# One 4 MB weight load of a mixture-of-experts kernel, made as a load of 96 rows and four loads of 8 rows

## What is computed

```python
D_MODEL, SEQ, N_EXPERTS, TOP_K, D_FF = 1024, 256, 32, 4, 1024

def moe_ffn(x, g_ffn, w_router, b_router, w_mlp1, b_mlp1, w_mlp2, b_mlp2):
    xt = rms_norm(x, g_ffn).reshape(N, D)
    logits = (xt @ w_router + b_router).astype(jnp.float32)
    top_v, top_e = lax.top_k(logits, TOP_K)
    wts = jax.nn.softmax(top_v, axis=-1).astype(x.dtype)
    ...
    def expert_block(args):
        xblk, e = args
        hdn = xblk @ w_mlp1[e] + b_mlp1[e]
        x_glu = jnp.minimum(hdn[:, ::2], SWIGLU_LIMIT)
        x_lin = jnp.clip(hdn[:, 1::2], -SWIGLU_LIMIT, SWIGLU_LIMIT)
        act = x_glu * jax.nn.sigmoid(SWIGLU_ALPHA * x_glu) * (x_lin + 1.0)
        return act @ w_mlp2[e] + b_mlp2[e]
    ...
    return x + y.reshape(B, S, D)
```

## Time and profile before

| | us |
|---|---|
| median of 3 runs | 1176.12 |
| lowest and highest of them | 1175.56, 1177.36 |
| the profiled execution | 1175.9 |
| its span (first to last instruction) | 1174.1 |
| PE busy in the span | 1126.4 (96%) |
| DVE, ACT, POOL busy | 399.8, 227.9, 26.8 |
| all DMAs | 454.37 MB, mean 387 GB/s |
| issue to landing of a 4 MB load (raw, median of 12) | 40.8 |

### The profile page before, as it was taken

One profiled execution on the slowest core, in us unless ns is written; L12 is line 12 of the kernel. 1 busy time (PEld: TensorE's weight loads), 2 busy tenths in 40 slices (PEclk: granted clock), 3 DMA queues, 4 the chain that ended last, 5 costly groups with the idle time before them and its releaser, 6 DMA issues.

```text
span 1174.1 us, 13010 instructions
## 1 busy us (share of the span) xinstructions
PE 1126.4 (96%) x5300; PEld 528.6 (45%) x5300; DVE 399.8 (34%) x664; ACT 227.9 (19%) x355; POOL 26.8 (2%) x38
## 2 busy tenths in 40 slices
PE   9999999999999999999999989999999999999998
PEld 8888788873333333333333333333333333333332
DVE  4765656753232222322322222222222222222221
ACT  3555557441000000101100000000000000000001
POOL 0001221010000000000000000000000000000000
PEclk9999999999999999999999999999999999999999
DMA  9866547998999999999999999999999999999995
GB/s 349 306 204 232 162 161 260 386 391 347 414 416 425 426 432 433 430 434 430 433 429 428 435 431 430 429 431 429 431 435 430 429 428 433 425 427 428 427 428 243
DMA packets 45633, 454.37 MB, mean 387 GB/s; under 512 B 3824, under 2 KB 4080, under 8 KB 27152
## 3 DMA queue, kind: packets, MB, share of 16 engines
q1 hardware_dynamic: 45008, 452.12, 92.9%
q10 hardware_dynamic: 576, 1.51, 0.3%
HBM read 452.56 MB, written 1.05 MB: 386 GB/s over the span
## 4 chain that ended last, share of the span: by engine, by line
PE 70%; DMA 29%; DVE 0%; issue 0%; ACT 0%; SPq 0%
PE PS L1733 23%; PE PS L1489 16%; PE PS L1740 13%; DMA gate_raw<-in_w_mlp 7%; DMA head_raw<-in_w_mlp 7%; DMA value_raw<-in_w_mlp 6%; DMA low_raw<-in_w_mlp 6%; DMA raw<-in_w_mlp 4%; PE PS L1776 3%; PE PS L1679 2%; PE PS L1456 1%; PE PS L1520 1%; PE PS L1763 1%; PE PS L1686 1%; PE PS L1429 1%; PE PS L1503 1%
## 5 line engine op out<-in xcount | busy, mean ns | idle before, releaser
L974 ACT ACTIVATE hT<-hT 128x512 f32<-128x512 f32 x31 | 19.5, 630 | 535.9 <-DVE hT L1389 535.9
L1389 DVE TENSOR_SCALAR hT<-PS 128x512 f32<-128x512 f32 x32 | 22.1, 692 | 296.8 <-PE PS L1733 296.8
L1733 PE MATMUL PS<-head_raw,XG 128*64 128x512 f32 x432 | 95.8, 595 | 4.3 <-DMA head_raw<-in_w_mlp 4.3
L1316 DVE TENSOR_TENSOR XG<-PS,gains 128x512 f32<-128x512 f32 x31 | 21.4, 692 | 225.0 <-PE PS L1686 225.0
L1733 PE MATMUL PS<-value_raw,XG 128*64 128x512 f32 x416 | 92.1, 595 | 3.0 <-DMA value_raw<-in_w_mlp 3.0
L1051 DVE TENSOR_TENSOR rest<-raw,mix_hi 128x2048 fp32r<-128x2048 f32 x35 | 80.2, 2291 | 43.0 <-ACT mix_hi L807 43.0
L1733 PE MATMUL PS<-low_raw,XG 128*64 128x512 f32 x400 | 89.0, 595 | 5.4 <-DMA low_raw<-in_w_mlp 5.4
L1733 PE MATMUL PS<-raw,XG 128*64 128x512 f32 x384 | 84.9, 595 | 4.5 <-DMA raw<-in_w_mlp 4.5
L1733 PE MATMUL PS<-gate_raw,XG 128*64 128x512 f32 x384 | 85.3, 595 | 3.1 <-DMA gate_raw<-in_w_mlp 3.1
L1328 DVE TENSOR_TENSOR hx<-hx,PS 128x512 f32<-128x512 f32 x116 | 72.2, 683 | 42.3 <-PE PS L1776 42.3
L807 ACT ACTIVATE mix_hi<-raw 128x2048 fp32r<-128x2048 f32 x35 | 67.0, 1914 | 40.3 <-PE PS L1489 26.2
(11 more groups left out here) (291 smaller groups left out, 1237.1 us busy)
## 6 DMA issues: line engine op xcount, KB each, us to landing
low_raw<-in_w_mlp SPq DMA_DIRECT2D x12, 4096.0 KB, 38.8
value_raw<-in_w_mlp SPq DMA_DIRECT2D x12, 4096.0 KB, 38.5
raw<-in_w_mlp SPq DMA_DIRECT2D x12, 4096.0 KB, 40.8
head_raw<-in_w_mlp SPq DMA_DIRECT2D x12, 4096.0 KB, 40.3
gate_raw<-in_w_mlp SPq DMA_DIRECT2D x11, 4096.0 KB, 40.3
value_raw<-in_w_mlp SPq DMA_DIRECT2D x14, 2048.0 KB, 25.4
low_raw<-in_w_mlp SPq DMA_DIRECT2D x14, 2048.0 KB, 25.5
head_raw<-in_w_mlp SPq DMA_DIRECT2D x13, 2048.0 KB, 14.0
```

Of the source, the lines that this page charges most:

```text
L974: act.activation(sig, glu, ACT.Sigmoid, scale=ALPHA).then_inc(sgm, 1)
L1316: dve.tensor_tensor(XG[:, :, :].rearrange("p (h c) s -> p h c s", h=2), banks[4].rearrange("p (c h s) -> p h c s", h=2, s=SL), rowgain.to_ ...
L1389: dve.tensor_scalar(glu, PS[:, 0:1024:2], LIMIT, None, ALU.min).then_inc(swi, 1)
L1733: mm = pe.matmul(PS[h * SL:(h + 1) * SL, n * 512:(n + 1) * 512], XG[:, 2 * u + c, :], parts[n].rearrange("p (q h r) -> p h q r", h=2, r=8) ...
```

## The change

The load `("up", 26, 2)`, 4 MB into the tile `raw`, is made by a new function, `load_w1_pair_uneven`: rows 0 to 95 in one DMA, which has the semaphore of the old one, and rows 96 to 127 in four DMAs of 8 rows each, which add to a new semaphore `uneven_in`. PE waits for both before `up(26, 2)`; `up(26, 3)` needs no new wait, since it comes later on PE. Nothing else is different, and all other loads and all arithmetic stay.

```diff
--- before.py
+++ after.py
@@ -85,6 +85,7 @@
 HALVES = [LOADS[LATER + i] for i in range(4)]
 HALF_RELEASED = FIRST[:4]
 PAIRS_END = 27
+UNEVEN = ("up", PAIRS_END - 1, 2)
 B2_BEFORE = LOADS[LATER + SLOTS_N]
 LAST_BANK = {(0, 0): 4, (0, 1): 3, (1, 0): 7, (1, 1): 5}
 SLOT = {load: HOMES[n] for n, load in enumerate(FIRST)}
@@ -413,6 +414,7 @@
 
         raw_in = [sem(f"raw_in{i}") for i in range(MIX_RING)]
         ring_in = [sem(f"ring_in{i}") for i in range(SLOTS_N)]
+        uneven_in = sem("uneven_in")
         half_used, half_in = sem("half_used"), [sem(f"half_in{i}") for i in range(len(HALVES))]
         first_half = {load: sem(f"first_half{i}") for i, load in enumerate(TWO_ROWS)}
         apart_in = {(load, c): sem(f"apart_in{i}{c}") for i, load in enumerate(APART) for c in range(2)}
@@ -545,6 +547,12 @@
 
             def load_w1_pair(e, u, pair, landed):
                 sp.dma_start(pair[:, :], w1[e, 256 * u:256 * u + 512, :].rearrange("e (p k) n -> p (e k n)", k=4)).then_inc(landed, 16)
+
+            def load_w1_pair_uneven(e, u, pair, landed):
+                rows = w1[e, 256 * u:256 * u + 512, :].rearrange("e (p k) n -> p (e k n)", k=4)
+                sp.dma_start(pair[0:96, :], rows[0:96, :]).then_inc(landed, 16)
+                for q in range(96, P, 8):
+                    sp.dma_start(pair[q:q + 8, :], rows[q:q + 8, :]).then_inc(uneven_in, 16)
 
             def load_w2_pair(e, pair, landed):
                 sp.dma_start(pair[:, :], w2[e, :, :].rearrange("e (p k) n -> p (e k n)", k=8)).then_inc(landed, 16)
@@ -693,7 +701,9 @@
                 used(held_before(n + in_pairs(load)))
                 tile, landed, _ = weight_tile(kind, j, u)
                 if in_pairs(load):
-                    if kind == "up":
+                    if load == UNEVEN:
+                        load_w1_pair_uneven(slice(j, j + 1), u, pairs[SLOT[load] // 2], landed)
+                    elif kind == "up":
                         load_w1_pair(slice(j, j + 1), u, pairs[SLOT[load] // 2], landed)
                     else:
                         load_w2_pair(slice(j, j + 1), pairs[SLOT[load] // 2], landed)
@@ -1718,6 +1728,8 @@
                     if load in TWO_ROWS:
                         pe.wait_ge(first_half[load], 16)
                     pe.wait_ge(landed, count)
+                    if load == UNEVEN:
+                        pe.wait_ge(uneven_in, 4 * 16)
                 for c in range(2):
                     if load in APART:
                         pe.wait_ge(apart_in[load, c], 32 if c == 0 else 16)
```

## The result

The changed kernel takes **1205.68 us** (median of 5 runs, 1201.4 to 1208.76); the kernel before, on the same chip, 1176.12 (median of 5, 1175.38 to 1179.24). The ratio is 1.0249, with a 95% interval of 1.0234 to 1.0264: 29.6 us slower. The forecast was 1192.5, with a range of 1177 to 1200. The direction was right, the size was not.

A forecast was written before the change was run, and what follows sets the result against it. Queued weight transfers were taken as the bound. On the serving engines 7.3 + 24.4 - 9.8 = 21.9 us, less a lead of 5.5, gave 16.4 us later: 1176.1 + 16.4 = 1192.5 us, range 1177 to 1200.

The forecast's parts named there:

- What bounds the kernel: From 906 us on, queued weight transfers at 429 GB/s are the bound; a delay reaches the end one for one.
- A row in an 8-row load, 4.9 to 6.1 us: In the four 8-row loads on eight engines, each 32 KB row takes this long; full rate is 1.22 us.
- The carry-over from 32 rows to 8: 32-row loads ran at half rate; in proportion 8 rows get an eighth, 54 GB/s, 19.5 us for the four loads.
- The 96-row load, 7.3 us or at most 9.8: Six rows per engine at 1.22 us, or 9.8 if 64 of the rows take only half the stream.
- The sum before the lead, 21.9 us: Extra time on the serving engines: 7.3 for 96 rows plus 24.4 for four 8-row loads, less 9.8 before.
- The subtraction of the lead, 5.5 us: Half the engines finish 4 to 7 us before the others; if they serve the 8-row loads, 5.5 us is covered.
- Issues on SP, 2.0 us, covered: Four more DMA issues at half a us each, hidden in the 10.7 us before SP's next issue, head_raw.
- The wait on PE near 997, 15 us or more: Sign in the profile after: one PE wait for raw of this length, where it had been 1.5 us.
- The plateau with the other half late: Sign at the end of the loads: half the engines busy for longer than 4 us, the former leading half now late.
- Balanced: Rival: 8-row loads at full rate on the leading half, landings 2.4 us earlier, 1173.7 us; chance 0.13.
- milder limit: Rival: a row in an 8-row load takes 2.4 us, end 1.8 us later, 1177.9 us; chance 0.07.
- wrong half: Rival: 8-row loads at full rate on the already late half, 2.4 us later, 1178.5 us; chance 0.04.

The follow-up runs named there:

- The early kernel: Changed kernel with the same uneven load made at item 8 instead of item 26: 1197.59 us, ratio 1.0195 to the kernel before.
- Alone: Loads-only kernel, no layer computed, each pattern awaited before the next: 128 rows 12.1 us, rows 0 to 95 16.8, four 8-row loads of neighbours 19.4.
- in line: Loads-only kernel, five 4 MB loads issued at once, the third changed: plain 51.1 us, with 96 rows and four 8-row loads 77.8.
- 96 + 32 rows: Changed kernel with one load of rows 96 to 127 in place of the four 8-row loads: 1193.31 us, ratio 1.0151 to the kernel before.
- the columns kernel: Changed kernel with its load as five loads of all 128 rows, half of each row, then four of 4 KB of each: 1175.83 us, ratio 0.9999.
- The last runs: Kernel before, load cut into every-fourth-row loads plus four or eight 8-row loads: rows 16 apart 1185.49, 1195.77 us; 4 apart 1181.84, 1186.29; sixteen, 16 apart, 1214.07.
- 64 + 64 rows: Kernel before with the load at item 26 made as rows 0 to 63 and rows 64 to 127: 1189.89 us, ratio 1.0122.
- the second series in line: Loads-only kernel, five 4 MB loads issued at once, the third as 96 rows and four 8-row loads: 77.8 us, 26.7 over plain.

## Why the prediction was wrong in size

- **What bounds the kernel**: right. The transfers do, and a delay goes to the end. The early kernel, with a wait of 2.3 us and a loss of 21, is the strongest proof.
- **A row in an 8-row load, 4.9 to 6.1 us**: right in kind and near in size. Alone 4.3 us (17.1/4), and 4.6 where all four go to the same rows; in line behind full loads 5.6, and in the profiled run some 3.8 (median of the 71 rows that start from 996 to 1012 us). The carry-over from 32 rows to 8, which the prediction named as its weak point, held to within a fifth or so.
- **The 96-row load, 7.3 us or at most 9.8**: wrong, and the first step that failed. It takes 14.5 us alone, six rows of 2.4 us on every engine. 96 rows were read as 128 rows less a quarter; a full rate was assumed where no row of the trace had shown one for less than 128 rows. This term alone makes 96 + 32 rows cost 10 us in line and 17.6 in the kernel, with no 8-row load at all.
- **The sum before the lead, 21.9 us**: by the times of the loads alone it would be 14.5 + 17.1 - 9.8 = 21.8. The same number, with one term too small by 7 and the other too large by 7; an accident. In line, where a row of an 8-row load takes 5.6 us, it is 14.5 + 22.3 - 9.8 = 27.0, and 26.7 was measured: there the 24.4 for the four loads is near, and the 7.3 for the 96 rows is what is missing.
- **The subtraction of the lead, 5.5 us**: wrong, the second step that failed. It held that the serving engines fall behind while the others go on. They don't go on at their rate: in the slow stretch the busy share stays at 9 and the rate is at a quarter to a half of full, and no row on any engine takes less than 2.3 us, even of the load ahead (46.7 us from issue to landing, where 41 was usual). In line every row on all 16 engines takes 5.6 us while the 8-row loads run. "The other half of the engines has work for longer than the delay, so it does not stop" was the sentence that made this mistake: it had work, but was slowed down as much. The lead itself was there and of about the size taken: before, the signals of the leading eight for `raw` came at 990.0 to 991.6 us, those of the late eight at 994.7 to 996.6. Which half serves was left open. In the profiled run it was neither: as far as the packets can be joined end to start, six of the eight serving engines are of the leading half and two of the late one. Without the subtraction the forecast would have been 1198; with 26.7, 1202.8, beside 1201.4 measured for the profiled run.
- **Issues on SP, 2.0 us, covered**: right; 1.36 us, covered, and the columns kernel confirms it.
- **The wait on PE near 997, 15 us or more**: right, 22.4, with 4.3 before it that were not foreseen. The 96-row load at its old time or earlier: wrong, 17 us later; the last 8-row load some 20 us after it: wrong, 10.5 us (1014.1 and 1024.6). The share at 1 with a low rate: right. The plateau with the other half late: wrong, there is none.
- **Balanced, milder limit, wrong half**: none of them occurred. The last runs show no form in which shifting rows between the halves gains anything, even with the rows spread. That the change might do nothing is excluded by the result.

What stays open: why a row of a 96-row load takes 2.4 us on every engine, and why the engines without rows of an 8-row load are slowed to its pace, which the runs show without a reason; and the 4 us between the profiled run and the median.

## What to carry to other kernels

A load should cover all 128 rows, and if it must be cut, by columns, or by every fourth row over the whole tile; both cost nothing here, while 96 + 32 or 64 + 64 rows cost 14 to 18 us for one 4 MB load. Few neighbouring rows hold up every transfer that is under way, so no lead or reserve elsewhere pays for them; in a kernel whose loads stand in line, count lost transfer, not waits. A term taken over at full rate because it looked harmless needs its row as much as the one under dispute.

## What the runs showed of the hardware

- Rows 0 to 95 take longer than rows 0 to 127: 16.8 against 12.1 us alone. Rows 0 to 111 do as well: issued at 223.00, the next pattern at 239.29, 16.3 us.
- While 8-row loads of neighbouring rows run among full loads, all 16 engines are busy (share 0.96) and together move 90 GB/s; with a 96-row load it is 218, with full loads 431 (the second series in line).
- Alone, 8 rows at a distance of 4 are at full rate (8.4 us for four loads), at 2, 8 or 16 at half of it (12.2 to 12.7), as neighbours at a quarter (19.4 to 20.6).
- In the profiled run of after the granted TensorE clock stood at 6 and 8 tenths in two slices, 9 or more elsewhere. PE had waited there 4.3 us and then 22.4; from 1014 to 1020 us, in the second wait, the granted clock is 0.50, the lower of its two levels (1.2 and 2.4 GHz). The 32 products after the first wait took 9.70 us and those after the second 9.03, instead of 7.09. The loads in the queue hid that: the rate was back at 393 to 439 GB/s from 1022.5 us on.
